# Half-wise combination of the dilated attention groups, copies ahead of exponentials, and second value halves moved from ScalarE to VectorE

## What is computed

```python
for gi, (window, dil) in enumerate(DIL_GROUPS):
    o_g, lse_g = _dilated_group(qb[:, :, hs], kb[:, :, hs], vb[:, :, hs], group_bias[gi],
                                dil, window // (2 * dil))
    outs.append(o_g)
    lses.append(lse_g)
wgt = jax.nn.softmax(jnp.stack(lses, axis=0), axis=0)
o_b = jnp.sum(wgt[..., None] * jnp.stack(outs, axis=0), axis=0)
...
merged = (gate_a * jnp.einsum('bsc,cd->bsd', o_a, w_branch_a[l])
          + gate_b * jnp.einsum('bsc,cd->bsd', o_b, w_branch_b[l]))
```

## Time and profile before

| | |
|---|---|
| median of 3 runs (lowest, highest) | 3305.85 us (3300.29, 3307.48) |
| the profiled execution's own time | 3304.23 us |
| its span | 3302.4 us |
| PE busy | 3110.5 us (94%) |
| DVE, ACT, POOL busy | 46%, 33%, 11% |
| stage 2 from its first value product to its last attention product | 1152.13 to about 1676.8 us |
| stage 3, from its first product | 1680.72 us |

### The profile page before, as it was taken

The page is one execution under the profiler, slowest core; times in us unless marked ns, Lnnn a source line. Parts: engine busy times, 40 slices in busy tenths (PEclk is TensorE's granted clock), DMA queues, the critical chain, the costliest instruction groups (busy, mean ns, idle before and its releaser), DMA issues.

```text
span 3302.4 us, 39261 instructions
## 1 busy us (share of the span) xinstructions
PE 3110.5 (94%) x16399; PEld 2589.9 (78%) x16399; DVE 1530.3 (46%) x2139; ACT 1074.1 (33%) x2309; POOL 363.3 (11%) x433
## 2 busy tenths in 40 slices
PE   7999999989999998999989999999999999997998
PEld 4788888877787876877768888888888876777887
DVE  4555656666653223121145345444444567532453
ACT  3443443444443223232321232122211234212453
POOL 0122232232221000000010000000000011001111
PEclk9999999999999999999999999999999999998899
DMA  2211111011111111111252321111111320101101
GB/s 107 65 48 49 38 55 49 26 39 33 33 42 61 53 44 46 42 42 49 102 202 90 143 68 58 51 52 39 51 52 51 98 91 26 64 29 45 37 27 39
DMA packets 59314, 192.78 MB, mean 58 GB/s; under 512 B 7649, under 2 KB 15329, under 8 KB 49922
## 3 DMA queue, kind: packets, MB, share of 16 engines
q1 hardware_dynamic: 58272, 189.19, 16.6%
q10 hardware_dynamic: 866, 1.09, 0.1%
HBM read 156.28 MB, written 33.98 MB: 58 GB/s over the span
## 4 chain that ended last, share of the span: by engine, by line
PE 80%; DVE 10%; ACT 5%; issue 2%; DMA 1%; POOL 0%; SPq 0%; ACTq 0%; DVEq 0%; POOLq 0%
PE ps L2356 19%; PE ps L2358 19%; PE ps L2357 19%; PE ps L2233 3%; PE ps L702 3%; PE ps L708 3%; PE ps L1692 2%; PE ps L3193 1%; DVE ar L1109 1%; PE ps L745 1%; PE ps L754 1%; PE ps L753 1%; PE ps L739 1%; PE ps L3252 1%; PE ps L1657 1%
## 5 line engine op out<-in xcount | busy, mean ns | idle before, releaser
L2356 PE MATMUL ps<-r,r 128*128 128x512 f32 (+4 forms) x2848 | 1136.4, 399 | 48.2 <-DVE r L230 12.2
L2358 PE MATMUL ps<-r,r 128*128 128x512 f32 (+4 forms) x2848 | 1072.8, 377 | 0.0
L2357 PE MATMUL ps<-r,r 128*128 128x512 f32 (+4 forms) x2848 | 1071.7, 376 | 0.0
L2356 PEld LDWEIGHTS ps<-r,r 128*128 128x128 f32 (+2 forms) x2848 | 545.3, 191 | 147.4 <-issue 24.4
L2358 PEld LDWEIGHTS ps<-r,r 128*128 128x128 f32 (+2 forms) x2848 | 542.6, 191 | 101.4
L2357 PEld LDWEIGHTS ps<-r,r 128*128 128x128 f32 (+2 forms) x2848 | 545.4, 191 | 82.6 <-issue 5.7
L2356 PE MATMUL ps<-r 128*128 128x512 f32 x512 | 199.7, 390 | 0.8 <-DVE r L2349 0.8
L2358 PE MATMUL ps<-r 128*128 128x512 f32 x512 | 199.3, 389 | 0.0
L2357 PE MATMUL ps<-r 128*128 128x512 f32 x512 | 199.2, 389 | 0.0
L2606 DVE TENSOR_TENSOR ar<-ar,ps 128x512 f32<-128x512 f32 x224 | 151.3, 686 | 92.6 <-PE ps L2358 92.4
L2344 ACT ACTIVATE r<-ar 128x2048 fp32r<-128x2048 f32 x48 | 91.7, 1910 | 260.8 <-PE ps L2358 254.4
(11 more groups left out here) (322 smaller groups left out, 4167.9 us busy)
## 6 DMA issues: line engine op xcount, KB each, us to landing
ar<-wst SPq DMA_DIRECT2D x72, 1024.0 KB, 4.8
ar<-wst SPq DMA_DIRECT2D x56, 512.0 KB, 3.9
ar<-x SPq DMA_DIRECT2D x16, 512.0 KB, 10.4
ar<-sc_g SPq DMA_DIRECT2D x32, 256.0 KB, 4.7
sc_h<-ar SPq DMA_DIRECT2D x32, 256.0 KB, 2.2
sc_x<-ar SPq DMA_DIRECT2D x16, 512.0 KB, 3.1
ar<-sc_x SPq DMA_DIRECT2D x16, 512.0 KB, 3.8
sc_b<-ar SPq DMA_DIRECT2D x24, 260.0 KB, 2.0
```

The source lines that it names most:

```text
L2356: t.do.matmul(o, l[0], r[0], start=first, stop=False)
L2357: t.do.matmul(o, l[0], r[1], start=False, stop=False)
L2358: return t.do.matmul(o, l[1], r[0], start=False, stop=last)
```

## The change

In the combination every step is split over two halves b of four row blocks: the transfers of `CBt` are six of half the size (half 0 of all groups first), the shares are computed for half 0 ahead of block 0 and for half 1 ahead of block 4, and so are ScalarE's three exponentials. In the attention ScalarE copies the turned probabilities of tile i ahead of the exponentials of tile i+1. The second half of each value piece is copied by VectorE. The signals are renamed to suit: the new copies tick `norm_out`, on which TensorE's first turn of a piece now waits.

```diff
@@ act_att
             for i in range(len(todo)):
-                if i + 1 < len(todo):
-                    logits(i + 1)
-                yield
                 yield
                 parts = todo[i][4]
...
                     a.do.activation(ov, iv_, ACT.Copy).then_inc(*att_pa.tick((g, i)))
                 yield
+                if i + 1 < len(todo):
+                    logits(i + 1)
+                yield
                 a.wait_ge(att_mm, (g, i, "u"))
@@ act_v
             for ct in range(4):
-                if ct:
-                    part(ct - 1, 1)
                 yield
...
-                part(ct, 0)
-                yield
-            part(3, 1)
+                part(ct)
+                yield
             yield
@@ dve_v
+            def half(ct):
+                key = ("v", g, ct, 1)
+                n = 512 // DIL[g]
+                v.wait_ge(dil_mm, key)
+                i = v_turn_keys.index(("v", g, ct, 0))
+                if i:
+                    v.wait_ge(turned, v_turn_keys[i - 1])
+                dv = Vs.rearrange("p (r l) -> p l r", r=DIL[g])[:, n:2 * n, :]
+                sv = bank(dil_keys.index(key) % 2).rearrange("p (l r) -> p l r", r=DIL[g])
+                v.do.tensor_copy(dv, sv).then_inc(*norm_out.tick(("half", g, ct)))
...
             for ct in range(4):
+                if ct:
+                    half(ct - 1)
                 for s in range(4):
...
+            half(3)
@@ act_cb
+            def exps(b):
+                for g in range(3):
+                    m = CBt[g][:, 4 * b:4 * b + 4, 512:516]
+                    a.wait_ge(cb_dve, (b, g))
+                    a.do.activation(m, m, ACT.Exp).then_inc(*cb_exp.tick((b, g)))
+
+            exps(0)
             yield
             for i in range(8):
+                if i == 4:
+                    exps(1)
@@ dve_cb
+            shares(0)
             for i in range(8):
                 if i:
                     yield
+                if i == 4:
+                    shares(1)
@@ pool_branches
-            p.wait_ge(cb_exp_in, "w")
             for i in range(8):
+                if i % 4 == 0:
+                    p.wait_ge(cb_dve, (i // 4, "w"))
@@ sp_branches
-            for g in range(3):
-                sp.do.dma_start(CBt[g], sc_b[g].rearrange("(i p) n -> p i n", p=P)).then_inc(*cb_in.tick(g))
+            for b, g in cb_keys:
+                sp.do.dma_start(CBt[g][:, 4 * b:4 * b + 4, :], sc_b[g][512 * b:512 * b + 512].rearrange("(i p) n -> p i n", p=P)).then_inc(*cb_in[b].tick((b, g)))
```

More of the change, by code:

```diff
@@ L1515, in program, with dil_out @@
         dil_mm = flow("dil_mm", dil_keys)
-        dil_ev = flow("dil_ev", dil_keys)
+        dil_ev = flow("dil_ev", [k for k in dil_keys if k[0] != "v" or k[3] == 0])
+        v_set_keys = [k for g in range(3) for ct in range(4) for k in [("half", g, ct)] + [("v", g, ct, k) for k in range(len(V_TURNS[g]))]]
+        def dil_out(en, key):
+            if key[0] == "v" and key[3]:
+                en.wait_ge(norm_out, ("half", *key[1:3]))
+            else:
+                en.wait_ge(dil_ev, key)
         gb_saved = [flow(f"gb_saved{q}", gb_keys[q::4], 16) for q in range(4)]
@@ L1730, in act_v, with part @@
             dil = DIL[g]
-            def part(ct, hf):
-                key = ("v", g, ct, hf)
+            def part(ct):
+                key = ("v", g, ct, 0)
                 n = 512 // dil
@@ L2033, in pe_cb @@
                 yield
-                t.wait_ge(cb_o, i)
+                t.wait_ge(cb_dve, ("o", i))
                 if i:
@@ L2098, in dve_cb, with shares @@
[L2098 to L2104 removed]
+            def shares(b):
+                bs = slice(4 * b, 4 * b + 4)
+                mb, zb, M, D = [m_[:, bs, :] for m_ in m], [z_[:, bs, :] for z_ in z], M4[:, bs, :], D4[:, bs, :]
+                v.wait_ge(cb_in[b], (b, 2))
+                v.do.tensor_tensor(M, mb[0], mb[1], ALU.max).then_inc(*dve_step.tick())
+                v.wait_ge(dve_step, dve_step.n)
+                v.do.tensor_tensor(M, M, mb[2], ALU.max).then_inc(*dve_step.tick())
+                v.wait_ge(dve_step, dve_step.n)
+                for g in range(3):
+                    v.do.tensor_tensor(mb[g], mb[g], M, ALU.subtract).then_inc(*cb_dve.tick((b, g)))
+                for g in range(3):
+                    v.wait_ge(cb_exp, (b, g))
+                    v.do.tensor_tensor(zb[g], zb[g], mb[g], ALU.mult).then_inc(*dve_step.tick())
+                v.wait_ge(dve_step, dve_step.n)
+                v.do.tensor_tensor(D, zb[0], zb[1], ALU.add).then_inc(*dve_step.tick())
+                v.wait_ge(dve_step, dve_step.n)
+                v.do.tensor_tensor(D, D, zb[2], ALU.add).then_inc(*dve_step.tick())
+                v.wait_ge(dve_step, dve_step.n)
+                v.do.reciprocal(D, D).then_inc(*dve_step.tick())
+                v.wait_ge(dve_step, dve_step.n)
+                for g in range(3):
+                    o = v.do.tensor_tensor(mb[g], mb[g], D, ALU.mult)
+                o.then_inc(*cb_dve.tick((b, "w")))
+                v.wait_ge(cb_dve, (b, "w"))
```

50 lines of the change are left out of this document (13 added, 37 removed).

## The result

The changed kernel takes 3257.12 us (median of 4 runs, 3256.20 to 3259.92), the kernel before 3303.83 us beside it (4 runs, 3300.29 to 3307.48): the ratio is 0.9862, with a 95% interval of 0.9850 to 0.9875. That is 46.7 us less. The prediction was 3270, in a range of 3259 to 3286: the direction is right, and the gain is larger than forecast, 1.9 us beyond the low end of the range.

What follows compares the result with a forecast made beforehand. TensorE was taken as the bound, so shorter waits shorten the run: 23.9 (attention) + 6.3 (combination) + 6 (clock) = 36.2 us off 3304.2 gives 3268.0, as a median 3269.6, stated as 3270; range 3259 to 3286 us.

Steps and rivals of the forecast that it cites:

- Waits of the attention: Attention: TensorE's waits on copies shrink by 11.0 us in group 0, 6.8 in group 1, 6.1 in group 2, 23.9 in all.
- The two places named in the prediction: Group 0, TensorE's waits of 3.07 and 5.75 us on ScalarE's copies of second value halves: about 1.0 and 3.8 us remain.
- the second halves on VectorE: Attention: VectorE copying second value halves directly behind the negation takes 2.0 and 1.9 us off two waits in group 0.
- VectorE's strided copy: Attention: VectorE's strided copy of a second value half from PSUM was taken to last 1.0 us.
- the slower rival: Attention: VectorE's strided write to `Vs` costs far more, deciding from 5.5 us per copy; 3318 us at 7 us; 4 in 100.
- The combination: Combination's first turn: shares start 6.3 us sooner, so TensorE's wait falls from 9.3 to 3.0 us.
- The rival in which both halves land together: Combination: half 0's transfers complete only with half 1's, so it gains 0 and the time is 3276 us; 12 in 100.
- At block 4: Combination: the second chain of shares adds up to 5.7 us on VectorE, against 5.2 us of cover; loss taken as 0.
- The clock: Attention, groups 0 and 1: at most 20.5 us lost to low granted clock; 6 us was taken to return with fewer waits.
- the clock's far end: Forecast's low end of 3256 us, with 20 us of clock returning; left out of the stated range.
- the anchor: Whole kernel: forecast counted from the profiled execution of 3304.2 us, with 1.6 us added to reach the median of the runs shown.

Runs made afterwards that it cites:

- the other profile with the old attention: Kernel before with only the combination split by halves, attention code unchanged: 3297.26 us, ratio 0.9979.
- the first experiment: Kernel before with only ScalarE's copy of tile i's turned probabilities moved ahead of the exponentials of tile i+1: 3265.65 us, ratio 0.9883.
- the full-clock measure: Changed kernel plus idle products ahead of four waits, 3251.48 us; its attention ran at full clock, its own products busy for 464.1 us.
- the best one: Kernel before with copies ahead and combination by halves, second halves left on ScalarE; 3256.86 us without idle products, 3248.93 us with them ahead of its waits.

## Why the prediction was right in kind and wrong in size

**Waits of the attention: right.** 23.9 us were forecast, 23.8 measured. That the two agree to 0.1 us is luck: against the other profile with the old attention (41.78 us idle) it would be 22.6. That the places agree is not. By groups it can be read from the stretches of the changed kernel that answer to the earlier trace rows, and the one behind them:

```profile
1193.60:1315.00 121.40, 110.68 (x577) 92.48 (x576) 44.49 (x55) 36.74 (x89) 0.00 (x0) 0.94 0.13 46
...
1387.00:1507.00 120.00, 116.63 (x575) 94.59 (x575) 37.94 (x47) 37.32 (x91) 0.00 (x0) 0.97 0.12 45
1507.00:1640.10 133.10, 128.05 (x644) 108.17 (x642) 25.12 (x31) 52.04 (x109) 0.00 (x0) 1.00 0.27 98
```

Length less busy time of TensorE: group 0 from 21.7 us to 10.7 (11.0 forecast to go, 11.0 gone), group 1 from 10.0 to 3.4 (6.8 forecast, 6.7 gone), the rest from 11.2 (1530 to 1680.72 us of before) to 5.0 (6.1 forecast, 6.1 gone). The two places named in the prediction wait 0.97 and 3.92 us, where about 1.0 and 3.8 had been said.

**To whom these waits belonged: wrong in one point.** The prediction gave the second halves on VectorE the 2.0 and 1.9 us of the places in the earlier trace rows. The copies ahead alone take 3.07 to nothing and 5.75 to 0.33 us, of which 1.63 us return at the next turn. The value halves, put beside them, take nothing away but set 5.8 us of waits on L1879 in place of 2.6 us on L1740 and 0.6 us on L1872: idle 19.1 and 19.3 us with them (two profiles), 16.6, 16.7 and 16.7 without (the kernels of the first experiment, of the copies with the combination, and its repeat). The sum was right because I had read the changed order row by row, in which the copy on VectorE does stand behind the negation; what I had not asked was how ScalarE's row would look with only one of the two edits. That the 2.5 us also appear in the total is likely but not shown: without the value halves 3254.99 and 3256.86 us, with them 3257.12 and 3260.39, and the intervals of the ratios overlap.

**VectorE's strided copy: right.** 1.0 us was taken; the eight with the stride take 1.02 to 1.09, the four of group 0 without it 0.69; the price at which the slower rival begins was 5.5.

**The combination: right.** 6.3 us forecast, 6.6 and 6.7 measured in the two profiles of the changed kernel; the turn waits 2.67 us for the forecast 3.0, and the shares start behind VectorE's finish. The rival in which both halves land together did not come about: half 0 was complete 3.0 us before the shares, as forecast (1708.8 against 1711.76). At block 4 nothing was lost: from the first turn at 1678.57 TensorE waits for nobody until 1738.3, and the 1.5 us there (on L2107) are in the kernel before too. Its wait of 0.9 us on L1595 is at 1664.69, ahead of the first turn, and is old as well.

**The clock: the step that failed.** The term was 6 us, "under a third" of 20.5, because "waits of 3 to 4 us remain, in each of which it may fall again". Measured on the same 2325 products, busy time falls by 12.3 us in one profile of the changed kernel and by 14.9 in the other (485.66 to 473.40 and 470.72). Waits of that length do remain, and the clock does fall behind them: those are the three stretches at 0.50 shown above, 20.4 us. What the term left out are the others. Of the nine stretches of the kernel before, six begin at or behind waits that the prediction itself counted as gone or cut to about 1 us (2.50, 2.58, 3.07, 1.87, 1.61 and 2.16 us, ending at 1215.9, 1250.0, 1264.3, 1430.5, 1496.8 and 1632.5). They last 23.8 us together, and at half clock that is 11.9 us lost, an estimate, made afterwards, that the trace of the kernel before allowed. The bound of 20.5 was well placed (by the full-clock measure the loss was 485.66 - 464.1 = 21.6 in all); "under a third" had no row behind it.

The loss is not simply in proportion to idle time. By the full-clock measure the kernel before loses 21.6 us with 42.9 us idle, the changed one 9.3 with 19.1 and 6.6 with 19.3, the copies with the combination 8.0 with 16.7, the copies ahead alone 9.8 with 16.6: 0.3 to 0.6 us for each us of idle time. But in the kernel with the value halves alone 5.7 us of idle time went and busy time stayed (486.27 us), in stage 3 of the changed kernel 6.7 us went and busy time stayed (139.26 and 139.33), and from 1530 us to the end of the old attention 11.2 us of idle time stand beside a granted clock of 0.99.

With 12 to 15 in place of 6 the sum is 42 to 45 us and the time 3261 to 3264 as a median. The measured gains of the changed kernel are 46.7 and 44.4. Its first profile is 47.2 us shorter than that of before: 36.05 in the attention, 6.60 in stage 3, and 4.57 in the first stage, whose code is the same. Its second is 44.0 us shorter: 38.57 and 6.66, less 1.2 us that the unchanged first and last stretches take more together. So the terms of the change come to 42.7 and 45.2 us, and the rest of either total is not its work.

**The range.** I left the clock's far end out from below, after having put the clock's most likely value too low; both errors point the same way. A third is in the anchor: 1.6 us were added because the three runs shown had a median of 3305.85 us, while 31 later runs of the kernel before have 3304.69 and the four beside the changed kernel 3303.83. The median missed the range by 1.9 us. Without the untouched first stage's 4.6 us in that profile it would have lain inside, so on which side of the edge it fell was partly chance; that the clock's term was at most half of what it measured was not.

## What to carry to other kernels

Cost the clock with the waits, and for each wait that goes, not only for the longest: list the stretches in which the granted clock is 0.50, find the wait ahead of each, and take half the length of those whose wait goes (11.9 us here, 12.3 and 14.9 measured). That is an estimate and not a rule: in the kernel with the value halves alone the stretch at 1264 us went with its wait, but one at 1277 us came, the one near 1301 us grew, and nothing was gained. The loss for each us of idle time (0.3 to 0.6 in this attention) is no substitute: 6.7 us less idle time in stage 3 brought no clock back. Where one copy waits behind another engine's work, ask first what happens if the order on its own engine is changed: here three moved lines gave 39.3 of 46.7 us, and moving the copy to a second engine beside that cost 2.5 us of idle time. Where a wait can't be removed, products that nobody reads can keep the clock up: 15.6 us in the kernel before, 7.9 in the best one, with no work made faster.

## What the runs showed of the hardware

- The granted clock can fall at short waits too. With 1.61 and 1.15 us of waiting within 6 us it was 0.74 over 20 us, a mix of the levels of 1.2 and 2.4 GHz, and 1.00 with the waits filled; I had counted on waits of 3 to 4 us. It does not always: around waits of 1.6 and 0.8 us it was 0.89 in one execution and 1.00 in another of the same kernel.
- In the attention idle time repeats to 0.2 us between two profiles of the changed kernel and among three with the copies ahead and the halves on ScalarE, but only to 1.2 us between two with the old attention; busy time repeats to 2.7, 1.7 and 3.3 us. Over the first 1150 us, with the same code, the length differs by up to 7.1 us. Two kernels should be compared by idle and busy time stretch by stretch before a few us are explained.
- VectorE's copy of 128x512 out of PSUM takes 1.02 us with a strided write and 0.69 without; ScalarE's takes 1.01 to 1.11 with the stride and 0.60 without.
- By the Trainium skill ("SBUF — State Buffer", "Who interferes with whom") a VectorE operation that reads both inputs from SBUF contends with a GpSimd operation that reads SBUF. The trace agrees again after the change: beside GpSimd's four products the weighted sum L2146 takes 1.41 us, and 0.69 once they are done. With GpSimd's work in two pieces of 5.8 and 5.9 us the same price is paid around each (L2146 takes 1.41 us again at 1708.51), and hidden at the second.
